# 122 products that nothing reads, put behind the last product of a one-core network kernel

## The chip, the cores and the metric

The kernel runs on one core of one Trainium2 chip (trn2). The metric is the device time of one execution in microseconds (us), lower is better; times are medians over runs. A profiled execution also gives a span, from its first to its last instruction.

## The reference

Two network blocks are applied one after the other to 256 rows of 1024 numbers in fp32: the first with four feed-forward parts, a recurrent/mLSTM mixer and a sparse attention mixer, the second with a pooling and retention mixer and then a feed-forward of 16384 experts. Only the end matters here:

```python
    hf = modulate(rmsnorm_2(x, lp['norm_ffn_g']), sh2, sc2)
    x = x + g2 * peer_ffn(hf, lp['peer_wq'], lp['peer_keys'], lp['peer_u'], lp['peer_v'])
...
    return rmsnorm_2(x, final_g)
```

`peer_ffn` picks 16 experts for each row and head, takes `gelu(u[e] . h)` times the softmax weight, and sums those multiples of `v[e]`. The kernel does it densely: it multiplies the rows by all experts' `u`, multiplies by a weight matrix that is zero where an expert wasn't picked, and multiplies by all `v`.

## The kernel before

The program is written engine by engine. Each stage adds work to the queues of SyncE (SP, which issues the DMAs), GpSimd (POOL), TensorE (PE), ScalarE (ACT) and VectorE (DVE), and semaphores order them. One block of such queues is open until the end of the kernel; `Kernel.close` (L396 to L402) closes it (L398), clears the semaphores (L400) and puts one more barrier (L401). At L398 each engine has a DRAIN, which ends when the engine's own work has ended, and then signals; POOL collects the signals of all the others and lets them go on.

An fp32 product is made of three (L539 to L545): each operand is split into a high and a low part of type fp32r, and `product` issues high by high, high by low and low by high. In the rows these are L543, L544 and L545, with moving operands of 256 or 512 columns against a stationary 128 x 128 piece. Before each product the stationary operand is loaded (LDWEIGHTS, engine PEld in the rows), also where it is the same as before. Products of plain fp32 operands (`mm`, L1041, and direct calls) stand in the trace as two records for one call. Transposes are products against an identity, `ident`.

`settle_pace` (L2116 to L2120) issues two products of the identity read as 16-bit numbers, start and stop set, into a bank whose content is not read. It is called at places of the expert stage and of two others. `start` begins with 12 products of `self.ones` in plain fp32 (L755), one behind the other into one place of bank 0, start and stop set, which nothing reads either.

The expert stage is `peer` (from L2609). It streams 256 half tiles (`experts`, 512 KB each) through three raw buffers; ACT makes the high part and POOL the low part of each in `high` and `low`, two slots of 1024 columns each. `up(n)` makes the 128 products with `u`, `down(n)` those with `v`, into PSUM banks 4 to 7. `GA` holds the high and low part of the weighted activations, two slots of 256 columns; `cells[0]` of the change is its high part. The last half tile goes to a place of its own (`last_tile`), and its low part is made by DVE (L3167).

After `down(125)` the queue of PE ends with a loop over the four output banks (t, h): for each of them the products of experts 126 and 127, and a signal `banked`. What follows is on the other engines: DVE multiplies a bank by the gate (L3173) and adds it to `keep_x` (L3177), ACT squares and sums it (L2996), small operations make the mean, root and reciprocal (L3182, L3186, L3001, L3191), DVE, POOL and ACT scale the rows (L3193, L2745, L3015), and SP stores them in four DMAs (L2730) and waits until they have landed. These use the banks 0 and 4 to 7 and the SBUF places of `x`, `g2`, `O1` and `O2`. Nothing on PE follows the loop over the banks, except its DRAIN at L398.

Of the kernel before, what the change touches and what calls it, by code (L numbers as in the profile page):

```python
# [16 lines left out]
F32 = mybir.dt.float32  # L17
F32R = mybir.dt.float32r
F16 = mybir.dt.float16
# [5 lines left out]
P = 128  # L25
# [94 lines left out]
class Modulation:  # L120
# [86 lines left out]
    def row(self, act, bank, row):  # L207

        self.k.nc.scalar.activation(row, bank[:, :], ACT.Copy).then_inc(self.copied.sem, 1)
# [118 lines left out]
class Kernel:  # L328
# [706 lines left out]
    def mm(self, out, lhsT, rhs, start, stop):  # L1035


        if isinstance(lhsT, (tuple, list)):
            ins = self.product(out, lhsT, rhs, start, stop)
        else:  # L1040
            ins = self.nc.tensor.matmul(out, lhsT, rhs, start=start, stop=stop)  # L1041
        if self.owed:
            self.owed -= 1
            ins.then_inc(self.released.sem, 1)
        return ins
# [1070 lines left out]
    def settle_pace(self, out):  # L2116

        square = self.ident.bitcast(F16)[:, 0:P]
        for _ in range(2):
            self.nc.tensor.matmul(out, square, square, start=True, stop=True)  # L2120

    def gate_row(self, part, banks):

        for k in range(KD):
            last = self.nc.tensor.matmul(self.psum[banks[k // 4]][:, (k % 4) * P:(k % 4 + 1) * P],
                                         self.modT[:, 8 * part + k, 0:1].to_broadcast([P, P]), self.ident,
                                         start=True, stop=True)
        return last
# [491 lines left out]
    def peer(self):  # L2620
# [4 lines left out]
        nc, ps, G, mod = self.nc, self.psum, G_PEER, self.modulation  # L2625
# [8 lines left out]
        high = side("high", 2 * D, dt=F32R).rearrange("p (s n) -> p s n", s=2)  # L2634
        low = side("low", 2 * D, dt=F32R).rearrange("p (s n) -> p s n", s=2)
# [7 lines left out]
        GA = [side(f"GA{n}", 2 * T, dt=F32R).rearrange("p (b t) -> p b t", b=2) for n in ("high", "low")]  # L2643
# [8 lines left out]
        at = lambda name, kb, cols: Arena(nc, f"peerT_{name}", self.ring_end + 1024 * kb - 64 * (kb >= 16), self.keep)(name, cols)  # L2652
# [95 lines left out]
        def _(pe):  # L2748
# [54 lines left out]
            w = self.ring_tile(pe, G_QUERY, 0)  # L2803
# [59 lines left out]
            for t in range(TT):  # L2863
                for h in range(2):
                    if t == 0:
                        pe.wait_ge(*made_low.at(4 * N - 3 + h))
                    for n in (N - 2, N - 1):
                        if t == 0 and n == N - 1:
                            pe.wait_ge(*last_low.at(h + 1))
                        last = self.product(ps[4 + 2 * t + h][:, :], [cell(i, n)[:, t * P:(t + 1) * P] for i in range(2)],  # L2870
                                            [halves_of(N + n, i)[:, h * 512:(h + 1) * 512] for i in range(2)], False, n == N - 1)
                    last.then_inc(banked.sem, 1)

        @self.block.scalar
        def _(act):
# [541 lines left out]
```

## Time and profile before

| | before |
|---|---|
| median of 2 runs | 2036.33 us (2035.77 and 2036.88) |
| span of the profiled execution | 2033.8 us |
| PE busy | 2017.6 us (99%), 15634 products |
| PEld busy | 1905.9 us (94%) |
| DVE, ACT, POOL busy | 52%, 56%, 85% |
| DMA | 395.28 MB, mean 194 GB/s |

The median lies 2.5 us above the span, time that is spent around the first and last instruction. A busy share says how long an engine had work in hand, not that it ran at its peak. Where products follow each other, one lasts longer than the distance to the next one's start, since they are pipelined: the distance of starts is what a stream costs, and the duration is what the last of it takes to come out. Times of a row are from the start of the span.

### The profile page before, as it was taken

Reading aid. Unit: us, or ns where it says so; the run is one execution under the profiler, and the core shown is the slowest. Engines: PE = TensorE matmul, PEld = TensorE weight load, DVE = VectorE, ACT = ScalarE, POOL = GpSimd, SP = SyncE. Lnnn points to the kernel's source line nnn. Section 1 sums busy time; section 2 is a strip of 40 time slices with the busy share of each in tenths; the row PEclk is TensorE's granted clock in tenths of the full one; section 3 lists DMA queues with packets and bytes.
Section 4 is the critical chain, followed back from the end, with each engine's and each line's share of the span. In section 5 each row is a group of like instructions: output and inputs, shape, how many; then the busy total and the mean of one; then the engine's idle time right before and its main releaser. Section 6 shows DMA issues by size and latency. Waiting matters only on the chain.

```text
span 2033.8 us, 39076 instructions
## 1 busy us (share of the span) xinstructions
PE 2017.6 (99%) x15634; PEld 1905.9 (94%) x15634; DVE 1057.5 (52%) x1985; ACT 1146.8 (56%) x1951; POOL 1718.8 (85%) x991
## 2 busy tenths in 40 slices
PE   9999999999999999999999999999999999999998
PEld 9999999999999979999889999999999998888886
DVE  6865745555454465224754316997788522223223
ACT  6344874445434475444654545557888655555555
POOL 5999789998999757899766686798777799999997
PEclk9999999999999999999999999999999999999999
DMA  9565456666666523666454455355454556555554
GB/s 350 210 222 190 166 187 249 217 219 246 248 250 225 208 83 138 239 223 220 166 181 145 149 185 196 124 190 177 167 167 167 165 185 203 193 195 193 193 196 146
DMA packets 80756, 395.28 MB, mean 194 GB/s; under 512 B 11100, under 2 KB 12252, under 8 KB 52448
## 3 DMA queue, kind: packets, MB, share of 16 engines
q1 hardware_dynamic: 80608, 393.28, 55.0%
q8 instruction: 97, 1.59, 0.3%
q14 instruction: 51, 0.42, 0.1%
HBM read 392.19 MB, written 1.05 MB: 193 GB/s over the span
## 4 chain that ended last, share of the span: by engine, by line
PE 89%; POOL 5%; DVE 3%; issue 2%; ACT 1%; DMA 1%; SPq 0%; ACTq 0%; POOLq 0%; DVEq 0%
PE bank L543 28%; PE bank L544 27%; PE bank L545 27%; POOL ring_low L496 5%; PE bank L1041 2%; PE bank L2782 1%; PE bank L2783 1%; PE bank L1828 1%; PE bank L1875 1%; PE bank L1857 1%; DMA ring_raw<-in_stream 1%; ACT ring_high L478 0%; DVE ring_low L981 0%; DVE keep_red L2482 0%; DVE context_red L2482 0%
## 5 line engine op out<-in xcount | busy, mean ns | idle before, releaser
L496 POOL TENSOR_TENSOR ring_low<-ring_raw,ring_high 128x1024 fp32r<-128x1024 f32 (+1 forms) x408 | 1026.5, 2546 | 191.6 <-ACT ring_high L478 189.7
L2740 POOL TENSOR_TENSOR peerS_low<-peerS_raw,peerS_high 128x512 fp32r<-128x512 f32 x510 | 659.5, 1318 | 85.2 <-ACT peerS_high L2892 83.7
L543 PE MATMUL bank<-keep_xThigh,ring_high 128*128 128x256 f32 x2080 | 582.6, 280 | 1.1 <-DVE ring_low L968 0.6
L545 PE MATMUL bank<-keep_xThigh,ring_low 128*128 128x256 f32 x2080 | 577.2, 278 | 0.0
L544 PE MATMUL bank<-keep_xTlow,ring_high 128*128 128x256 f32 x2080 | 577.2, 277 | 0.0
L478 ACT ACTIVATE ring_high<-ring_raw 128x2048 fp32r<-128x2048 f32 x204 | 390.1, 1913 | 265.4 <-PE bank L545 245.6
L543 PEld LDWEIGHTS bank<-keep_xThigh,ring_high 128*128 128x128 f32 x2080 | 390.9, 188 | 4.6 <-issue 3.7
L544 PEld LDWEIGHTS bank<-keep_xTlow,ring_high 128*128 128x128 f32 x2080 | 391.9, 188 | 0.3
L545 PEld LDWEIGHTS bank<-keep_xThigh,ring_low 128*128 128x128 f32 x2080 | 391.0, 188 | 0.0
L2892 ACT ACTIVATE peerS_high<-peerS_raw 128x512 fp32r<-128x512 f32 x510 | 320.5, 629 | 119.8 <-PE bank L545 92.4
L543 PE MATMUL bank<-keep_xThigh,peerS_high 128*128 128x256 f32 x1024 | 287.9, 281 | 0.0
L544 PE MATMUL bank<-keep_xTlow,peerS_high 128*128 128x256 f32 x1024 | 284.3, 278 | 0.0
L545 PE MATMUL bank<-keep_xThigh,peerS_low 128*128 128x256 f32 x1024 | 284.1, 277 | 0.0
L3137 DVE TENSOR_TENSOR peerS_GAlow<-peerA_A,peerS_GAhigh 128x256 fp32r<-128x256 f32 x127 | 90.1, 710 | 252.5 <-ACT peerS_GAhigh L2924 252.5
L544 PE MATMUL bank<-peerS_low,peerS_GAhigh 128*128 128x512 f32 x508 | 197.9, 390 | 0.0
L545 PE MATMUL bank<-peerS_high,peerS_GAlow 128*128 128x512 f32 x508 | 197.9, 390 | 0.0
L543 PE MATMUL bank<-peerS_high,peerS_GAhigh 128*128 128x512 f32 x508 | 197.9, 390 | 0.0
L543 PEld LDWEIGHTS bank<-keep_xThigh,peerS_high 128*128 128x128 f32 x1024 | 192.7, 188 | 0.3
L544 PEld LDWEIGHTS bank<-keep_xTlow,peerS_high 128*128 128x128 f32 x1024 | 192.9, 188 | 0.0
L545 PEld LDWEIGHTS bank<-keep_xThigh,peerS_low 128*128 128x128 f32 x1024 | 192.4, 188 | 0.0
L994 DVE TENSOR_TENSOR bank<-bank,keep_R 128x512 f32<-128x512 f32 x44 | 30.8, 700 | 245.3 <-PE bank L545 245.1
L933 ACT ACTIVATE ffn_silu<-bank 128x512 f32<-128x512 f32 x44 | 26.4, 599 | 166.6 <-DVE bank L994 166.6
(562 smaller groups left out, 3800.4 us busy)
## 6 DMA issues: line engine op xcount, KB each, us to landing
ring_raw<-in_stream SPq DMA_DIRECT2D x215, 1024.0 KB, 4.8
peerS_raw<-in_experts SPq DMA_DIRECT2D x256, 512.0 KB, 3.6
modcols_w<-in_ada_cols SPq DMA_DIRECT2D x32, 512.0 KB, 5.8
modlate_w<-in_ada_cols SPq DMA_DIRECT2D x8, 512.0 KB, 5.7
modcols_rows<-in_cond_rows SPq DMA_DIRECT2D x3, 1024.0 KB, 6.9
start_x<-in_x SPq DMA_DIRECT2D x2, 512.0 KB, 4.3
ring_raw<-in_stream SPq DMA_DIRECT2D x4, 256.0 KB, 5.8
context_in<-in_ctx SPq DMA_DIRECT2D x1, 1024.0 KB
```

The source lines that it names most:

```text
L478: self.nc.scalar.activation(self.parts(n)[0][:, cut], self.raw_slot(n)[:, cut], ACT.Copy).then_inc(self.high_done.sem, 1)
L496: self.nc.gpsimd.tensor_tensor(low_[:, cut], self.raw_slot(n)[:, cut], high[:, cut].bitcast(F32), ALU.subtract).then_inc(done.sem, 1)
L543: mm(out, sh, mh, start=start, stop=False)
L544: mm(out, sh, ml, start=False, stop=False)
L545: return mm(out, sl, mh, start=False, stop=stop)
L933: s_.activation(sg, pair(i, 0), ACT.Silu).then_inc(silu.sem, 1)
L994: v_.tensor_tensor(pair(i, 0), pair(i, 0), over, ALU.mult).then_inc(scaled.sem, 1)
L1041: ins = self.nc.tensor.matmul(out, lhsT, rhs, start=start, stop=stop)
L1828: last = nc.tensor.matmul(ps[4 + b][:, 0:P] if t == 0 else ps[4 + b][:, P:384], qT[rows, c, t * P:(t + 1) * P], kT[br][rows, c // 4, 0:(t ...
L2740: g_.tensor_tensor(low[:, m % 2, cut], xraw[:, m % 3, cut], high[:, m % 2, cut].bitcast(F32), ALU.subtract).then_inc(made_low.sem, 1)
L2892: s_.activation(halves_of(m, 0)[:, cut], xraw[:, m % 3, cut], ACT.Copy).then_inc(made_high.sem, 1)
L3137: v_.tensor_tensor(cell(1, n), A[:, n, :], cell(0, n).bitcast(F32), ALU.subtract).then_inc(gal.sem, 1)
```

## The change

Behind the loop over the output banks, PE gets 122 more products. Each sets start and stop and writes bank 1 or 2, which nothing reads from there on; nothing waits for them and they wait for nothing. They read `high`, `low`, `GA` and `ident` as they stand. Counted from the diff: five rows of 8 products with 512 moving fp32r columns (in order; two slots in turns in blocks of 16 columns; in turns in blocks of 4; every second column; the same two columns 256 times), 8 products of 16-bit numbers with 256 columns, six rows of 10 with 256 fp32r columns that begin at column 0, 4, 16, 32, 64 and 128 of `high`, one row of 10 with a stationary operand out of `low`, and 4 products in plain fp32 with 256 columns.

```diff
+    def unread_products(self, cells, high, low):
+
+
+        ps, mm = self.psum, self.nc.tensor.matmul
+        w = cells[0][:, 0, 0:P]
+        flat = high.rearrange("p s n -> p (s n)")
+        two = high.rearrange("p s (b c) -> p b s c", c=16)[:, 0:16]
+        lines = high.rearrange("p s (b c) -> p b s c", c=4)[:, 0:64]
+        ident = self.ident.bitcast(F16)
+
+        def row(count, out, weights, moving):
+            for _ in range(count):
+                mm(out, weights, moving, start=True, stop=True)
+
+        row(8, ps[1][:, :], w, flat[:, 0:512])
+        row(8, ps[2][:, :].rearrange("p (b s c) -> p b s c", s=2, c=16), w, two)
+        row(8, ps[1][:, :].rearrange("p (b s c) -> p b s c", s=2, c=4), w, lines)
+        row(8, ps[2][:, :], w, flat[:, 0:1024:2])
+        row(8, ps[1][:, :], w, flat[:, 0:2].unsqueeze(1).to_broadcast([P, 256, 2]))
+        row(8, ps[2][:, 0:256], ident[:, 0:P], ident[:, 0:256])
+        for at in (0, 4, 16, 32, 64, 128):
+            row(10, ps[1 + at // 4 % 2][:, 0:256], w, flat[:, at:at + 256])
+        row(10, ps[1][:, 0:256], low[:, 0, 0:P], flat[:, 0:256])
+        row(4, ps[2][:, 0:256], w.bitcast(F32), flat[:, 0:256].bitcast(F32))
...
                     last.then_inc(banked.sem, 1)
+            self.unread_products(GA, high, low)
```

## Rows read from the trace of the kernel before

**Rows 1.** The page: busy time, share of the span, instructions; chain by engine and line
```profile
PE 2017.6 (99%) x15634; PEld 1905.9 (94%) x15634; DVE 1057.5 (52%) x1985; ACT 1146.8 (56%) x1951; POOL 1718.8 (85%) x991
...
PE 89%; POOL 5%; DVE 3%; issue 2%; ACT 1%; DMA 1%; SPq 0%; ACTq 0%; POOLq 0%; DVEq 0%
```

**Rows 2.** Timeline of the end: start us, us, engine line op out<-in
```profile
2024.36 0.40 PE L544 MATMUL bank<-peerL_last,peerG_GA3high 128*128 128x512 f32 x1
...
2024.37 0.69 DVE L3177 TENSOR_TENSOR keep_x<-keep_x,bank 128x512 f32<-128x512 f32 x1
2024.59 0.40 PE L545 MATMUL bank<-peerL_last,peerG_GA3low 128*128 128x512 f32 x1
...
2025.77 0.75 DVE L3177 TENSOR_TENSOR keep_x<-keep_x,bank 128x256 f32<-128x256 f32 x2
...
2028.04 1.33 ACT L3015 ACTIVATE keep_x<-keep_x,keep_stat 128x512 f32<-128x512 f32 x2 [0.16 <-issue]
```

**Rows 3.** Source view of L398, the block's end: duration ns min/median/max, first and last start us
```profile
L398 PEldq DRAIN  x1: 4358/4358/4358, 2020.7 to 2020.7; - x1
...
L398 SPq DRAIN  x1: 7/7/7, 2032.4 to 2032.4; - x1
```

**Rows 4.** SP's own waits from 2015 us on: us in total, times, longest
```profile
SPq L398 <- DMA out<-keep_x: 2.1, 1, 2.1
```

**Rows 5.** PE alone in three stretches: busy (x instructions), granted clock, DMA share, GB/s
```profile
28.00:48.00 20.00, 20.00 (x171) 1.00 0.88 325
...
575.00:650.00 75.00, 75.00 (x664) 1.00 0.65 233
...
1750.00:1950.00 200.00, 200.00 (x884) 1.00 0.59 194
```

**Rows 6.** Timeline of PE, 1602 to 1604 us: 16-bit products, then fp32r ones
```profile
1603.19 0.22 PE L2783 MATMUL bank<-peerU_col,peerU_low 128*128 128x128 f16 x1
1603.24 0.22 PE L2782 MATMUL bank<-peerU_col,peerU_high 128*128 128x128 f16 x1
1603.30 0.22 PE L2783 MATMUL bank<-peerU_col,peerU_low 128*128 128x128 f16 x1
1603.33 0.36 PE L543 MATMUL bank<-keep_xThigh,peerS_high 128*128 128x256 f32 x1
1603.53 0.28 PE L544 MATMUL bank<-keep_xTlow,peerS_high 128*128 128x256 f32 x1
1603.65 0.28 PE L545 MATMUL bank<-keep_xThigh,peerS_low 128*128 128x256 f32 x1
```

**Rows 7.** Timeline of PE, 1116 to 1119 us: products in plain fp32
```profile
1116.68 1.03 PE L1041 MATMUL bank<-mix_vn_vn,mix_PTb_PTb 128*128 128x256 f32 x4
1117.54 1.03 PE L1041 MATMUL bank<-mix_S_S,mix_qd_qd 128*128 128x256 f32 x4
```

**Rows 8.** Groups of PE and PEld by line and shape: count, busy us, mean ns
```profile
L543 PE MATMUL bank<-keep_xThigh,ring_high 128*128 128x256 f32 x2080 | 582.6, 280 | 1.1 <-DVE ring_low L968 0.6 <-DVE keep_xTlow L3073 0.5
...
L545 PE MATMUL bank<-peerS_high,peerS_GAlow 128*128 128x512 f32 x508 | 197.9, 390 | 0.0
...
L2798 PE MATMUL bank<-peerT_xs_xs,keep_ones 128*128 128x256 f32 x16 | 3.7, 386 | 0.3 <-ACT peerT_xs_xs L2928 0.3
...
L2120 PE MATMUL bank<-keep_ident 128*128 128x128 f16 x24 | 3.4, 223 | 0.0
```

**Rows 9.** Tile views of two stationary operands of 64 columns, PEld: ns min/median/max
```profile
L1041 PEld LDWEIGHTS bank<-ring_raw,nsa_cmpX0first x16: 193/196/219, 690.7 to 693.8; 128*64 128x64 f32 x16
...
L1875 PEld LDWEIGHTS bank<-nsa_PT,nsa_vv x128: 132/137/138, 739.2 to 776.9; 128*64 128x64 f32 x128
```

**Rows 10.** Engines in two stretches of the end: busy (x), then PEclk, DMA share, GB/s
```profile
2018.00:2025.00 7.00, 6.30 (x27) 4.45 (x25) 6.43 (x10) 1.86 (x5) 2.55 (x2) 1.00 0.00 0
2025.00:2027.00 2.00, 0.00 (x0) 0.00 (x0) 1.93 (x7) 1.53 (x6) 1.05 (x1) 1.00 0.00 0
2027.00:2034.00 7.00, 0.00 (x0) 0.00 (x0) 1.52 (x5) 1.73 (x5) 0.22 (x1) 0.68 0.40 151
```

**Rows 11.** Timeline of PE, first 8 us and 1608 us: plain fp32, 128 columns
```profile
1.07 4.99 PE L755 MATMUL bank<-keep_ones 128*128 128x128 f32 x24 [1.07 <-POOL keep_ones L746]
...
1608.86 1.95 PE L2125 MATMUL bank<-keep_ident,keep_modT 128*128 128x128 f32 x16
```

**Rows 12.** Groups of PEld by line and shape: count, busy us, mean ns
```profile
L544 PEld LDWEIGHTS bank<-peerS_low,peerS_GAhigh 128*128 128x128 f32 x508 | 95.4, 188 | 19.6
...
L2782 PEld LDWEIGHTS bank<-peerU_col,peerU_high 128*128 128x128 f16 x256 | 24.2, 97 | 1.1
```

## The prediction

> **What bounds the kernel now.** I read the page first: PE is busy 99% of the span and holds 89% of the chain that ended last [rows 1]. So over the whole kernel nearly every product on PE's queue costs its own distance. But the change puts its products where PE has nothing more to do, so what counts is the end, and there I read the timeline and the block's end. The last product starts at 2024.59 and lasts 0.40 us [rows 2]. PE's DRAIN at L398 starts at 2020.7 and lasts 4.358 us, so PE is done at 2025.1 [rows 3]. The others are not: DVE adds the last pieces from 2025.77 on, ACT scales rows until 2028.04 + 1.33 = 2029.4 [rows 2], and SP then waits 2.1 us for the stores to land [rows 4]. SP's DRAIN ends at 2032.4 [rows 3], and it is the last of the five. From there to the end of the span are 2033.8 - 2032.4 = 1.4 us of barrier and semaphore clearing, which begin only when the last engine has drained, whichever that is. PE therefore has a free stretch of 2032.4 - 2025.1 = 7.3 us. What it does beyond that moves the end one for one.
>
> **The change part by part.** Nothing is removed or moved, and no wait, DMA or work on another engine is added; no queue but PE's gets an instruction, and on PE nothing stands behind the new products but the DRAIN. The cost is the stream of 122 products, less 7.3 us. The distance of starts is what each costs:
>
> - 512 columns of fp32r. In a long run of such products 884 records touch 200 us [rows 5]; two of them only reach in at the edges, so 200/882 = 0.227 us each. At the end of the kernel, after DVE's late low part, they stand a little wider: from 2024.36 to 2024.59 is 0.23 us [rows 2]. The wider pace also shows for 256 columns, where 20 us at the start of the kernel hold 171 records, 0.118 us each, against 75/662 = 0.1133 in the long run [rows 5], a factor of 1.04. The new products follow the last ones without a gap, so I take the wider pace, 0.231: 40 x 0.231 = 9.24 us.
> - 8 products of 16-bit numbers, 256 columns. With 128 columns starts lie 0.055 us apart, 1603.19 to 1603.24 to 1603.30 [rows 6]; twice the columns, 0.111: 0.89 us. The step back to fp32r costs something once: that product starts at 1603.33 and the next only at 1603.53, 0.20 instead of 0.12 [rows 6]. 0.09 us.
> - 70 products of 256 columns of fp32r, six rows at different beginnings and one with another stationary operand. After 16-bit products the kernel before runs at the narrow pace (that is what `settle_pace` is called between), so 70 x 0.1133 = 7.93 us [rows 5]. At the wide pace it would be 8.3. Which columns of a buffer a contiguous read starts at is something the kernel before varies all the time, in both operands, at one mean duration of 277 to 280 ns [rows 8]. I take no surcharge for it.
> - 4 products in plain fp32, 256 columns. L2798 is called 8 times and stands as 16 records [rows 8], so a call is two. Four records go from 1116.68 to 1117.54, 0.215 each [rows 7]. 8 x 0.215 = 1.72 us.
>
> The sum is 9.24 + 0.89 + 0.09 + 7.93 + 1.72 = 19.9 us, of which 7.3 lie under the tail of the others: +12.6 us. PE drains at 2025.1 + 19.9 = 2045.0, and the span goes from 2033.8 to 2046.4. The median of the runs stands 2.5 us above the span of the profiled execution, and its two runs 1.1 us apart; the same step from the median gives 2036.33 + 12.6 = 2048.9 us, or +0.6%.
>
> **What the trace does not show** is a moving operand that isn't contiguous; all that I see on PE are plain runs. Four of the five rows of 512 columns are not: blocks of 16, blocks of 4, every second column, two columns over and over. The nearest row is a strided stationary operand. `nsa_cmpX0first` is loaded in 64 columns that lie 8 numbers apart and takes 196 ns, against 137 ns for 64 columns in a row [rows 9]: 59/64 = 0.92 ns for each column that isn't beside the one before. As an upper bound I let each break in a moving operand cost that. Every second column: 512 breaks, 0.47 us a product, 3.8 for 8. Two columns over and over: 256 breaks, 1.9. Blocks of 4: 128 breaks, 0.9. Blocks of 16: 32 breaks, 0.2. Together 6.8 us, and 2055.7 us in all. The lower bound is a little under the sum, since a read of two columns over and over could also be spared whatever makes an fp32r product 0.227 long where one of plain fp32, which streams as many steps in two passes of 256 columns, takes 0.215 [rows 5, 7]: 40 x 0.016 = 0.6 us less, 2048.3. I take no surcharge, since breaks alone do not make the price: a contiguous load of 128 columns takes 188 ns and one of 64 takes 137 [rows 12, 9], 0.8 ns a column, while a contiguous moving operand runs at 0.227/512 = 0.44 ns a column [rows 5]. The two paths have different rates, and the moving one must be fed faster anyhow. But both ends stay in the range.
>
> The Trainium skill has a rule on this (Advanced Engine Details and Errata, Memory Cachelines): SBUF is read in lines of 16 bytes, and two hits in a line are enough for the full rate. By it the strided load of the 64 columns, one hit a line, should be slow, and the trace agrees (196 against 137 ns); all moving patterns of this change have two hits or more, and the sum would stay as it is. A reading of the same rule by which two hits are just half of what a moving operand needs makes the second rival below.
>
> **The rivals.**
>
> 1. *The stream at the rates above*: 2048.9 us, and with small errors of the pace (0.4 us), of the switch between types and of the median (0.6 us) 2047.6 to 2050.2. For it: every rate is from long runs of the same kernel, and PE waits for nobody. 0.64.
> 2. *Reads that fetch anew cost more.* The row of every second column takes twice its time, 8 x 0.231 = 1.8 us more (2050.7), perhaps that of the two repeated columns too (2052.6), and by the upper bound 2055.7. For it: the strided load [rows 9]. Against it: the moving path's own rate. 0.24.
> 3. *The clock falls.* The granted clock is 1.00 as long as PE works and the mean over 2027 to 2034, where PE has been idle since 2025, is 0.68 [rows 10], a fall from 2.4 to 1.2 GHz. In the first microseconds 24 records take 4.99 us, 0.21 each, where later 16 of the same shape take 1.95, 0.11 each [rows 11]. If the clock were low throughout, the stream would be 39.8 us, +32.5, 2068.8 us. Against it: the new products follow the old without a gap, so PE doesn't idle. 0.05.
> 4. *The change does nothing*, because products whose result isn't read are dropped or because they hide. Time 2036.3. Against it: the 24 unread products of L2120 stand in the trace [rows 8], and 19.9 is well over 7.3. 0.04.
> 5. *The other side, over 2% slower: products do not overlap when each starts a bank anew.* The new ones overwrite the same bank 8 or 10 times in a row, and should each have to wait for the last to come out before it loads its weights, each would cost load and duration: 40 x (0.188 + 0.390) = 23.1, 70 x (0.188 + 0.277) = 32.6, 8 x about 0.37 = 3.0 for the 16-bit ones (0.097 + 0.220 for 128 columns, and 0.05 for the others), 8 x (0.190 + 0.380) = 4.6; 63.3 us in all [rows 8, 12], +56.0, 2092.3 us. It passes 2% (40.7 us) when the stream takes 48.0 us, 0.39 us a product. Against it: L755 does just that, and its 24 records in 4.99 us leave no room for load and duration one behind the other [rows 11]. 0.02.
>
> Left over is 0.01, for which I can name nothing and which I give to faster.
>
> **How the numbers follow.** The likeliest is the first: 2048.9 us. Its own range is 2047.6 to 2050.2. The range for 8 in 10 takes in the lower bound and most of the second rival, to short of its far end: 2047.4 to 2054.0. Two per cent is about what a measurement of this kernel can tell from no change. Rivals 1 to 4 lie within it (0.6%, 1% at the most, 1.6%, 0): 0.97. Slower by more is the fifth, 0.02; faster 0.01.
>
> **What would show it.** In the profile of the changed kernel PE should be busy to about 2044.8 with no gap behind 2024.6, and PE's DRAIN at L398 should end last, near 2045.0, while SP's has still ended at about 2032.4. PE and PEld should have 118 + 8 = 126 records more, 15760. The starts in the five rows of 512 columns should all lie 0.231 us apart; the second rival shows in the fourth and fifth, where they would be near 0.46, or a few hundredths wider in the third. After the 16-bit row the distances should be 0.113, the same for all six beginnings. The granted clock should stay 1.00 until some microseconds behind 2045. DVE, ACT and POOL should have the times that they had: in the tail before, DVE's L3177 took 0.69 us beside PE at work [rows 2], and 12 us of cover now lie over them.
>
> The prediction is wrong if a kind of product costs more than its row here says, which its starts would show, or if the end of the block costs more when PE comes last than when SP does; the distance from PE's DRAIN to the end of the span, 1.4 us here, would show that.

## The result and the profile after

The changed kernel takes 2051.35 us (median of 2 runs, 2049.3 and 2053.39) against 2036.33 before: a ratio of 1.0074, interval 1.0058 to 1.009. The span of its profiled execution is 2047.5 us, 13.7 above the 2033.8 of before. By the line of 2% nothing has changed; by its own interval the kernel is slower by some 15 us.

First the page's busy line, which answers to [rows 1]:

```profile
PE 2038.7 (100%) x15760; PEld 1922.5 (94%) x15760; DVE 1067.1 (52%) x1985; ACT 1146.9 (56%) x1951; POOL 1722.1 (84%) x991
```

The block's end, source view of L398 (duration ns min/median/max, first and last start us), for [rows 3]:

```profile
L398 SPq DRAIN  x1: 7/7/7, 2031.3 to 2031.3; - x1
L398 PEldq DRAIN  x1: 3092/3092/3092, 2043.0 to 2043.0; - x1
```

SP's own waits (us in total, times, longest), for [rows 4]:

```profile
SPq L398 <- PEq L398: 14.9, 1, 14.9
...
SPq L398 <- DMA out<-keep_x: 2.1, 1, 2.1
```

126 records have come, as many as 118 products and 4 calls of two records make. SP has drained at 2031.3 as it did before, 7.8 us after the start of the last product of the loop (2023.55, below; 2024.59 and 2032.4 before, [rows 2, 3]). PE drains at 2043.0 + 3.1 = 2046.1, and SP now waits 14.9 us for it. From there to the end of the span are 1.4 us, as before. In this execution the loop ended 1.0 us earlier than in the one of before, for no reason that the change holds (the queue up to there is the same), which is why the spans are 13.7 apart and the stream less its cover, below, 14.8.

The timeline of PE shows that the new products follow without a gap. Behind it are the stretches, which give what each row costs. They are cut at the first start of each row of the change: in order, blocks of 16, blocks of 4, every second column, two columns over and over, 16-bit, the 70 of 256 columns, plain fp32. Columns are busy us (x records touched), granted clock, DMA share, GB/s; the length of a stretch is the row's cost.

```profile
2023.55 0.39 PE L545 MATMUL bank<-peerL_last,peerG_GA3low 128*128 128x512 f32 x1
2023.78 11.29 PE L2134 MATMUL bank<-peerS_high,peerS_GAhigh 128*128 128x512 f32 x40
2034.90 1.05 PE L2134 MATMUL bank<-keep_ident 128*128 128x256 f16 x8
2035.71 7.39 PE L2134 MATMUL bank<-peerS_high,peerS_GAhigh 128*128 128x256 f32 x60
...
2044.13 1.89 PE L2134 MATMUL bank<-peerS_high,peerS_GAhigh 128*128 128x256 f32 x8
```

```profile
2023.78:2025.62 1.84, 1.84 (x8) 1.00 0.00 0
2025.62:2027.54 1.92, 1.92 (x9) 1.00 0.16 63
2027.54:2029.54 2.00, 2.00 (x9) 1.00 0.68 256
2029.54:2033.13 3.59, 3.59 (x9) 1.00 0.30 118
2033.13:2034.91 1.78, 1.78 (x10) 1.00 0.00 0
2034.91:2035.71 0.80, 0.80 (x10) 1.00 0.00 0
2035.71:2044.13 8.42, 8.42 (x73) 1.00 0.01 2
2044.13:2045.86 1.73, 1.73 (x10) 1.00 0.00 0
sum 22.08, PE 22.08; mean PE 2.76
```

The stream is 22.1 us, not 19.9. 1.75 us of the difference are one row, every second column. (A product counts as touched in two stretches where it reaches over the cut, so the counts add up to more than 126.)

### The profile page after: what moved, and what is told of

It reads as the page before. It is cut to its first block, busy times and chain, and to the rows that moved or that the text cites. A ratio compares the mean times of both kernels' runs of the same rounds, so it can differ in the third digit from the quotient of the medians.

```text
span 2047.5 us, 39328 instructions
## 1 busy us (share of the span) xinstructions
PE 2038.7 (100%) x15760; PEld 1922.5 (94%) x15760; DVE 1067.1 (52%) x1985; ACT 1146.9 (56%) x1951; POOL 1722.1 (84%) x991
## 4 chain that ended last, share of the span: by engine, by line
PE 87%; POOL 7%; DVE 2%; issue 2%; ACT 1%; DMA 1%; SPq 0%; POOLq 0%; DVEq 0%; ACTq 0%
PE bank L543 26%; PE bank L545 26%; PE bank L544 26%; POOL ring_low L496 5%; POOL peerS_low L2765 3%; PE bank L1041 2%; PE bank L2134 1%; PE bank L2807 1%; PE bank L2808 1%; PE bank L1828 1%; PE bank L1875 1%; PE bank L1857 1%; ACT ring_high L478 0%; DVE ring_low L981 0%; DMA ring_raw<-in_stream 0%
## 5 line engine op out<-in xcount | busy, mean ns | idle before, releaser
L3163 DVE TENSOR_TENSOR peerS_GAlow<-peerA_A,peerS_GAhigh 128x256 fp32r<-128x256 f32 x127 | 99.5, 784 | 244.0 <-ACT peerS_GAhigh L2950 244.0
```

Of the source, the lines that this page charges most:

```text
L3163: v_.tensor_tensor(cell(1, n), A[:, n, :], cell(0, n).bitcast(F32), ALU.subtract).then_inc(gal.sem, 1)
```

## The experiments

Where distances of starts are given with three decimals, they are the usual difference between neighbouring starts in that row; (n - 1) of them and the duration of the last make up the length of the merged row that is shown. `lines`, `lines2`, `pace` and `regions` were executed once each; they are read by these distances and not by their total times. The ratios are the measurement's own, over all its executions, and can differ in the fourth decimal from that of the two medians.

**The free stretch.** 28 products in order in place of the 122:

```diff
-        row(8, ps[1][:, :], w, flat[:, 0:512])
...
-        row(4, ps[2][:, 0:256], w.bitcast(F32), flat[:, 0:256].bitcast(F32))
+        for _ in range(28): mm(ps[1][:, :], w, flat[:, 0:512], start=True, stop=True)
```

> Only 28 products of 512 columns in order in place of the 122. At 0.231 us each the stream is 6.5 us long, less than the 7.3 us for which PE has drained before SP. Theory A, free stretch: PE's DRAIN at L398 ends before SP's, the span is that of the kernel before within 0.3 us, and the ratio to before is 1.000 within its interval. Rival: unread products beside the tail slow DVE, ACT or the stores, or PE's stream costs from its first product on: +1 us or more, up to 6.5 (ratio 1.0005 to 1.003).

Measured: 2037.86 us against 2037.38 for the kernel before in the same comparison, a ratio of 1.0004, interval 0.9995 to 1.0013. Its timeline and the block's end:

```profile
2026.53 0.39 PE L545 MATMUL bank<-peerL_last,peerG_GA3low 128*128 128x512 f32 x1
2026.77 6.53 PE L2127 MATMUL bank<-peerS_high,peerS_GAhigh 128*128 128x512 f32 x28
```

```profile
L398 PEldq DRAIN  x1: 4242/4242/4242, 2029.1 to 2029.1; - x1
...
L398 SPq DRAIN  x1: 7/7/7, 2034.3 to 2034.3; - x1
```

28 products last 6.5 us and are gone before SP has drained, 7.8 us behind the start of the last product of the loop, as in the trace before (2034.3 and 2026.53 here): the theory of the free stretch holds. PE's DRAIN ends at 2029.1 + 4.2 = 2033.3, 1.0 us before SP's. The interval would not have shown a cost of 1 us, but the tail between the two starts is the same length, and that shows that none of it was slowed.

That length is not fixed, though. It is 7.8 us in eight of the ten traces, but 9.6 in `pace` (2034.7 - 2025.03) and 9.7 in `regions` (2033.2 - 2023.51), two runs described below. In both, SP waits 3.9 and 4.0 us for the stores to land where it waits 2.1 in the others, and in both a transfer of 16 KB of instructions (queue q8) comes while the stores are under way, beside one of 8 KB that every trace has there. SP's wait in `pace`, and the queue of that transfer in the window from 2030 to 2035 us (packets, MB, share of 16 engines):

```profile
SPq L398 <- DMA out<-keep_x: 3.9, 1, 3.9
```

```profile
...
q8 instruction: 1, 0.02, 1.2%
```

In the changed kernel the 16 KB come at 2036 us, behind the stores (they are the 2 GB/s in the stretch from 2035.71 on), and `short` has none behind its loop. So the cover of 7.3 us held for the changed kernel, but another stream of products can stretch it: PE is done 0.5 us after the loop's last start, and in these two the cover was 9.1 and 9.2 us, with a tail 1.9 us longer for all. That the transfer makes the stores late is read from these two coincidences and not tested.

**The same again, twice over, and without the dear row.** `again` is the changed kernel with more runs; the other two:

```diff
             self.unread_products(GA, high, low)
+            self.unread_products(GA, high, low)
```

```diff
-        row(8, ps[2][:, :], w, flat[:, 0:1024:2])
```

> The changed kernel once more, with more rounds. Its stream is 22.1 us long in the trace, so the step from before should be 22.1 - 7.3 = 14.8 us less what varies in where the last product of the loop starts (1.0 us earlier in the changed kernel's trace): 13.8 to 14.8 us, ratio 1.0068 to 1.0073. Rival: the step of 15.0 us between the medians of two runs each (1.0074) holds something beside the stream, and the ratio is 1.0078 or more.

> The 122 products twice. One for one beyond the free stretch: the stream is 44.2 us, the step from before 44.2 - 7.3 = 36.9 us, ratio 1.0181. If the end of the block had a cost of its own when PE comes last, or the first microseconds of the stream were dearer, the step would differ from twice 22.1 less 7.3 by that. If the clock fell in it, it would be longer by up to 22 us for each 22 us at the low clock.

> The changed kernel without its fourth row, the 8 products of every second column. The row took 3.6 us in the trace. Theory A (the row costs what its starts say): PE's DRAIN ends 3.6 us earlier relative to the last product of the loop, the stream is 18.5 us, and the step from before 11.2 us, ratio 1.0055. If the row only cost what a row in order does (1.85 us) and the rest came from elsewhere, the step would be 12.9 us, ratio 1.0063.

| | stream by theory | ratio by theory | ratio measured | PE drained behind the loop's last start |
|---|---|---|---|---|
| again | 22.1 us | 1.0068 to 1.0073 | 1.0073 (1.0059 to 1.0087) | 22.5 us |
| double | 44.2 | 1.0181 | 1.0182 (1.0165 to 1.0199) | 44.5 |
| no_step | 18.5 | 1.0055 | 1.0052 (1.0035 to 1.0069) | 18.9 |

The last column is PE's DRAIN less the start of the loop's last product, in us of each trace: 2045.1 + 3.1 - 2025.67 for `again`, 2067.0 + 3.1 - 2025.55 for `double`, 2039.8 + 3.1 - 2024.02 for `no_step`, and 2046.1 - 2023.55 = 22.5 for the changed kernel. The second helping of 122 products adds 22.0 us, one for one, with the clock at 1.00; the row of every second column is worth 3.6. `double` also settles whether the stores, which move during the rows of blocks and of every second column, made these dear: in the second helping no store is left, and the rows take 1.92, 2.00 and 3.59 us again. The interval of `no_step` (7 us wide) holds the rival's 1.0063 as well, and that of `again` its rival's 1.0078; it is the traces that decide. Against something beside the stream in `again` speak its DRAIN, 22.5 us behind the loop's last start, with 1.5 us from there to the end of its span (2049.7 - 2048.2). Loops that end at 2023.55 in one execution and at 2026.53 in another, in the same code, say why a median of a few can't: that spread, 3.0 us, is nearly as large as the row.

**What a moving operand costs by its pattern.** In place of the 122 products, rows of 8 (or 4 calls in plain fp32) that differ in what is moved; some of the lines:

```diff
...
+        for _ in range(8): mm(ps[2][:, :], w, flat[:, 2:514], start=True, stop=True)
+        for _ in range(8): mm(ps[1][:, :].rearrange("p (a b) -> p a b", b=2), w, pairs, start=True, stop=True)
+        for _ in range(8): mm(ps[1][:, :], w, flat[:, 0:1536:3], start=True, stop=True)
+        for _ in range(8): mm(ps[2][:, :], w, flat[:, 0:2048:4], start=True, stop=True)
+        for _ in range(8): mm(ps[1][:, 0:256], w, flat[:, 0:2048:8], start=True, stop=True)
...
+        for _ in range(8): mm(ps[2][:, :], ident[:, 0:P], some(8, 16), start=True, stop=True)
```

> In place of the 122 products: 12 rows of 8 with moving operands of other patterns (fp32r, then 16-bit), and 3 rows of 4 in plain fp32. What is read is the distance of starts in each row. Theory A, groups: the moving operand comes in aligned groups of four fp32 numbers (16 bytes), and a product takes the larger of its columns' time and about 1.76 ns for each group that it has to fetch (0.450 us over 256 groups in the changed kernel). Per product: in order 0.231; in order from the third number on 0.231; two of each four 0.45; blocks of four that lie across two groups 0.45; step 3 (384 groups) 0.68; step 4 (512) 0.90; step 8 with 256 columns 0.45; one column over and over 0.22; 16-bit in order 0.22, step 2 (128 groups) 0.22 to 0.25, step 4 (256) 0.45, step 8 (512) 0.90; plain fp32 records of 256 columns: in order 0.216, step 2 (128 groups) 0.22, step 4 (256) 0.45. Theory B, breaks: each column that isn't beside the one before costs 0.43 ns more, wherever it lies. Then: two of each four 0.34; blocks of four across two groups 0.25 as in the changed kernel; steps 3 and 4 0.45 like step 2; step 8 with 256 columns 0.23; one column over and over 0.45; 16-bit steps 2, 4 and 8 all 0.43.

The timeline of PE in `lines`, one merged row for each kind, in the order of the expectation: in order, from the third number on, two of each four, blocks of four across two groups, steps 3, 4 and 8, one column over and over, 16-bit steps 1, 2, 4 and 8, plain fp32 steps 1, 2 and 4:

```profile
2026.65 2.00 PE L2136 MATMUL bank<-peerS_high,peerS_GAhigh 128*128 128x512 f32 x8
2028.48 2.04 PE L2137 MATMUL bank<-peerS_high,peerS_GAhigh 128*128 128x512 f32 x8
2030.36 3.79 PE L2138 MATMUL bank<-peerS_high,peerS_GAhigh 128*128 128x512 f32 x8
2033.96 2.84 PE L2139 MATMUL bank<-peerS_high,peerS_GAhigh 128*128 128x512 f32 x8
2036.63 3.77 PE L2140 MATMUL bank<-peerS_high,peerS_GAhigh 128*128 128x512 f32 x8
2040.22 3.86 PE L2141 MATMUL bank<-peerS_high,peerS_GAhigh 128*128 128x512 f32 x8
2043.90 1.92 PE L2142 MATMUL bank<-peerS_high,peerS_GAhigh 128*128 128x256 f32 x8
2045.65 1.93 PE L2143 MATMUL bank<-peerS_high,peerS_GAhigh 128*128 128x512 f32 x8
2047.41 1.90 PE L2144 MATMUL bank<-keep_ident 128*128 128x512 f16 x8
2049.15 1.97 PE L2145 MATMUL bank<-keep_ident 128*128 128x512 f16 x8
2050.96 3.77 PE L2146 MATMUL bank<-keep_ident 128*128 128x512 f16 x8
2054.55 7.38 PE L2147 MATMUL bank<-keep_ident 128*128 128x512 f16 x8
2061.75 3.60 PE L2148 MATMUL bank<-peerS_high,peerS_GAhigh 128*128 128x256 f32 x8
2065.14 2.41 PE L2149 MATMUL bank<-peerS_high,peerS_GAhigh 128*128 128x256 f32 x8
2067.38 3.77 PE L2150 MATMUL bank<-peerS_high,peerS_GAhigh 128*128 128x256 f32 x8
```

Neither theory stands. Theory A (groups of four, a price for each) is right for two of each four (0.451 for 0.45), for one column over and over (0.219), for the 16-bit rows (0.226, 0.451, 0.900) and for plain fp32 in steps 2 and 4 (0.226, 0.451), and wrong for steps 3 and 4 in fp32r (0.450 and 0.460 for 0.68 and 0.90), for step 8 (0.218 for 0.45) and for blocks across two groups (0.331 for 0.45). Theory B (a price for each break) has steps 3, 4 and 8 of fp32r right and 16-bit step 4 nearly (0.43 for 0.451), and pairs (0.34), blocks across groups (0.25), one column over and over (0.45) and 16-bit steps 2 and 8 (0.43 each) wrong. So the second run tested whether it goes by the kind of number, or whether the small operand of the 16-bit rows, read up to 16 times, made them dear:

```diff
+        for _ in range(8): mm(ps[1][:, :], w16, half[:, 0:2048:4], start=True, stop=True)
+        for _ in range(8): mm(ps[2][:, :].rearrange("p (a b) -> p a b", b=32), w, again, start=True, stop=True)
...
+        for _ in range(8): mm(ps[2][:, :], w16, half[:, 0:4096:8], start=True, stop=True)
+        for _ in range(40): mm(ps[1][:, 0:256], w, flat[:, 0:256], start=True, stop=True)
```

> In place of the 122 products: rows of other moving operands, to mend what the run of read patterns left. There fp32r products of 512 columns took 0.45 us for steps 2, 3 and 4 alike, but 16-bit ones 0.226, 0.451 and 0.900 for steps 2, 4 and 8, over a small operand read 4 to 16 times. Theory C, kind: in fp32r a step costs double whatever its size, and in 16-bit the time goes with the bytes stepped over from 8 bytes on (16 bytes a column: 0.90), because 16-bit numbers are taken in other portions. Then 16-bit steps 2, 4, 8 over a long operand are again 0.226, 0.451, 0.900, and fp32r step 4 over 128 columns read 16 times is 0.46. Theory D, the small operand: reading the same few hundred bytes again is what costs, and the long 16-bit row of step 8 is 0.45 while the fp32r row over 128 columns is 0.90. Further rows: fp32r step 16 with 128 columns 0.11 by C; blocks of four aligned columns, four left out, 0.25 as the alternating blocks of the change; pairs that lie across two groups of four 0.45 (a group each) to 0.90; plain fp32 records with 256 columns in order 0.216, step 2 0.226, step 4 0.451. The clock: in that run it fell to 1.2 GHz from 4 us after the start of the 0.900 row on, and the plain fp32 records behind it took 0.427. If a stream of starved products lowers it, it falls here too during or behind the row of step 8, the 40 products of 256 columns behind it take 0.213 us at first and 0.120 later, and the plain fp32 rows, which here stand in front, take 0.216.

The rows of `lines2` that decide, by its timeline: plain fp32 in order, step 2 and step 4; fp32r step 4 over 128 columns, 16 times; 16-bit step 8 over 4096 numbers; then 40 products in order.

```profile
2026.65 1.89 PE L2134 MATMUL bank<-peerS_high,peerS_GAhigh 128*128 128x256 f32 x8
2028.37 1.98 PE L2135 MATMUL bank<-peerS_high,peerS_GAhigh 128*128 128x256 f32 x8
2030.19 3.77 PE L2136 MATMUL bank<-peerS_high,peerS_GAhigh 128*128 128x256 f32 x8
...
2040.52 4.28 PE L2140 MATMUL bank<-peerS_high,peerS_GAhigh 128*128 128x512 f32 x8
...
2051.99 7.36 PE L2145 MATMUL bank<-peerS_high,keep_ident 128*128 128x512 f16 x8
2058.31 6.94 PE L2146 MATMUL bank<-peerS_high,peerS_GAhigh 128*128 128x256 f32 x40
```

The small operand is not it: the long 16-bit row of step 8 stands at 0.900 again and the small fp32r one at 0.461. The theory of the kind of number holds. Put as the cost of one column at the high clock (distance over columns; a plain fp32 call is two records, here one of them):

| bytes from column to column | 2 | 4 | 8 | 12 | 16 | 32 | 64 |
|---|---|---|---|---|---|---|---|
| 16-bit, ns | 0.42 | 0.44 | 0.88 | | 1.76 | | |
| plain fp32, ns | | 0.84 | 0.88 | | 1.76 | | |
| fp32r, ns | | 0.44 | 0.88 | 0.88 | 0.90 | 0.85 | 0.88 |

At the steps measured, plain fp32 and 16-bit cost the larger of the column's own time and 0.11 ns for each byte stepped over. fp32r doubles with the first step and stays there. Why fp32r stops at 0.88 and the others don't, the runs do not say; the others were not tried beyond 16 bytes. The last entry is weaker than the rest: its products have only 128 columns (0.113 us each), there is no row in order of that size beside it, and each has a load of weights of 0.19 us in its time, which may set the distance as well. Blocks in fp32r: pairs cost 0.88 a column wherever they lie (0.451 for two of each four, 0.453 for pairs across two groups). Four aligned with four left out cost 0.233 a product (0.25 expected), no more than a row in order, though blocks of four in turns from two slots cost 0.250 and, across groups, 0.331.

**The clock.** PEclk in `lines2`: in front of the 0.900 row, in its first part, in its later part, at the first and at the later ones of the 40 products:

```profile
2046.00:2050.00 4.00, 4.00 (x13) 1.00 0.00 0
2052.00:2054.80 2.80, 2.80 (x6) 1.00 0.00 0
2054.90:2057.90 3.00, 3.00 (x4) 0.51 0.00 0
2058.50:2061.70 3.20, 3.20 (x13) 0.50 0.00 0
2061.90:2062.70 0.80, 0.80 (x9) 1.00 0.00 0
```

As in `lines` (below), the granted clock goes from 1.00 to 0.50 (2.4 to 1.2 GHz) inside the row of step 8, while PE is busy for all of it by the records. In `lines` that row goes from 2054.55 to 2061.75:

```profile
2058.00:2061.00 3.00, 3.00 (x5) 0.70 0.00 0
2061.00:2064.00 3.00, 3.00 (x8) 0.50 0.00 0
```

The products of that row keep their 0.900 at both levels, so it is not the array's clock that paces them, and the operand is the likely cause; the 256-column ones behind it take 0.213 at the low level and 0.118 to 0.124 after it. In `lines` the plain fp32 records behind that row took 0.427, in `lines2`, ahead of it, 0.216. Rows at 0.45 did not lower it: in `lines` fp32r steps 3, 4 and 8, all at 0.85 to 0.90 ns a column, follow each other for 9.0 us (2036.63 to 2045.65) with the clock at 1.00. That the slow row itself lowers the clock rests on two falls in two runs, and on none in the traces that lack such a row; no run varies its length.

**Why 0.120 and not 0.113.** `pace` and `regions` put rows of 256 columns behind a `settle_pace` pair:

```diff
+        pair()
+        for n in range(20): mm(ps[2][:, 0:256], w, flat[:, 0:256], start=True, stop=True)
...
+        for n in range(10): mm(ps[1][:, 0:256], own, x, start=True, stop=True)
```

> In place of the 122 products: rows of 10 or 20 fp32r products with 256 columns, most behind a pair of 16-bit products of 128 columns (the kernel's own settle_pace). Asked is why the rows behind the 16-bit ones stood 0.120 us apart in the changed kernel where the kernel's long runs have 0.1133. Theory A, the pair: two 16-bit products of 128 columns bring the narrow distance within a few products, and eight with 256 columns did not. Then all rows behind a pair run at 0.1133 after at most five products, and only the first row, without a pair, at 0.118 to 0.120. Theory B, the stream: products of one kind with one stationary operand that start their bank anew keep 0.118 to 0.120 behind a pair too, and one of the rows that come closer to the kernel's own products (two banks in turns, summing up in one bank, two stationary operands in turns, stationary out of high with moving out of xT, moving operands of other places) comes down to 0.1133 and names what it hangs on. Theory C, chance of the phase: rows differ without a pattern.

Measured: behind a pair the rows come to 0.120, as the row without one does, and stay there for 20 products. Two banks in turns, summing up, two stationary operands in turns and other places in `high` change nothing. Only the row with `high` stationary and `xT` moving came down, to 0.113 from its sixth product on. That is theory B, with the place of the operands as what it hangs on, and `regions` took the places apart:

```diff
+        for n in range(16): mm(ps[2][:, 0:256], far, flat[:, 0:256], start=True, stop=True)
+        pair()
+        for n in range(16): mm(ps[1][:, 0:256], far, x, start=True, stop=True)
```

> In place of the 122 products: seven rows of 16 fp32r products of 256 columns, each behind a settle_pace pair, with the stationary and the moving operand in the lower part of the memory (high, GA) or in the upper one (xT). Theory A, one stream apart: the distance is 0.1133 when the two operands lie in different parts and 0.120 when in the same, so high with xT, xT with high, GA with xT and xT with GA come to 0.1133, and xT with xT, GA with high and high with high stay at 0.120. Theory B, the moving operand: rows that move xT come to 0.1133 (high, xT and GA as stationary), all that move high or GA stay at 0.120, whatever is stationary. Theory C, the one buffer: only high as stationary with xT moving, the pair of the kernel's own products, comes to 0.1133.

Its timeline: `high` with `xT`, `xT` with `high`, `xT` with itself, `GA` with `xT`, `GA` with `high`, `high` with itself, `xT` with `GA` (stationary first):

```profile
2023.84 2.13 PE L2132 MATMUL bank<-keep_xThigh,peerS_high 128*128 128x256 f32 x16
...
2025.90 2.13 PE L2134 MATMUL bank<-peerS_high,keep_xTlow 128*128 128x256 f32 x16
...
2027.97 2.15 PE L2136 MATMUL bank<-keep_xThigh,keep_xTlow 128*128 128x256 f32 x16
...
2030.06 2.13 PE L2138 MATMUL bank<-keep_xThigh,peerS_GAhigh 128*128 128x256 f32 x16
...
2032.13 2.15 PE L2140 MATMUL bank<-peerS_high,peerS_GAhigh 128*128 128x256 f32 x16
...
2034.22 2.16 PE L2142 MATMUL bank<-peerS_high 128*128 128x256 f32 x16
...
2036.31 2.13 PE L2144 MATMUL bank<-peerS_GAhigh,keep_xTlow 128*128 128x256 f32 x16
```

The split is that of theory A: operands in different parts of the memory stand at 0.118 in the end, operands in the same part at 0.120. But the place isn't all, for in the changed kernel the rows that begin at columns 16 and 32 stand at 0.118 too, with both operands in the same part. And theory A's number failed: none of the four rows reached 0.1133 within 16 products, the very pair that did in `pace` included. What brings a stream to the narrow distance is open. It is worth 0.007 us a product, 0.5 us here.

## Why the prediction was right, and where not

- *PE's stream decides, less what lies under the tail.* Right, and shown from both sides: 28 products cost nothing that can be seen, 244 cost twice the stream less the same cover. With the measured stream the step is 22.1 - 7.3 = 14.8 us; measured were 15.0 (two runs each), and in `again` a ratio of 1.0073, 14.9 us, with 14.2 between the medians (2051.55 and 2037.38).
- *512 columns in order, 9.24 us for 40 at one price.* The price held for the row in order (1.85 predicted, 1.84 measured) and for what repeats two columns (1.78). Blocks of 16 cost 1.92, blocks of 4 2.00. The step that failed is "I take no surcharge" for every second column: 3.59 for 1.85. My reason, that the moving path must be fed faster than the stationary one, was true for reads in order and said nothing about steps. The second rival had this very time for that row (1.8 us more) and was wrong about the repeated columns and about its upper bound (3.8 more). The lower bound's 0.016 us a product is 0.231 less 0.215; with the 0.227 of its sentence it would be 0.012.
- *Page and measurement.* The rule that I cited from the Trainium skill (Advanced Engine Details and Errata, Memory Cachelines), two hits in a line of 16 bytes for the full rate, does not hold for TensorE's moving fp32r operand: every second column has two hits in a line and takes 0.450 us for 0.231. The measurement decides. Nor does it for 16-bit numbers 8 bytes apart, which have two hits as well and take 0.451 for 0.216. It holds for 16-bit numbers 4 bytes apart (0.226), which have four, and for plain fp32 8 bytes apart (0.226 for 0.216 a record), which have two.
- *70 products of 256 columns, 7.93 us, with 0.09 for the change of type.* 8.42 measured, 0.118 to 0.120 each in place of 0.1133; the term was too small by 0.4 us. I had tied the narrow pace to the 16-bit products in front, and `pace` shows that these don't bring it. That the beginning of a contiguous read costs nothing worth counting was right: the first of the seven rows took 1.28 us, with the change of type, and the others 1.18 to 1.20. The 0.09 for that change were for nothing here: the last 16-bit product is followed after 0.027 us and the first fp32r one after 0.201, together what 0.109 and 0.120 make.
- *16-bit, 0.89 us, and plain fp32, 1.72.* 0.80 and 1.73.
- *The other engines keep their times, and the block's end costs 1.4 us whoever is last.* Right. Beside the new products DVE's last L3177, now L3203, takes 0.76 us for two halves (0.75 before), ACT's L3015, now L3041, 1.35 (1.33), and POOL's L2745, now L2770, 1.30 (1.27). DVE's total is 9.6 us more, but 9.4 of that are the low part of `GA` (L3137, now L3163: 0.784 us each for 0.710), all ahead of the change.
- *The median's 2.5 us above the span.* The profiled execution of the changed kernel took 2049.3 us, 1.8 above its span, and so do those of `again` and `double` (1.7 and 1.8). The rest of my 2.5 was the scatter of the runs, and the same scatter is why a step of 14.8 and one of 13.7 in the spans are no contradiction.
- *Two products that overwrite a bank don't overlap* fell as expected: in `pace` the row that sums up in one bank and the rows that start anew both stand at 0.120.

So the direction, the mechanism and the range were right; of the 2.2 us by which the stream was longer, 1.75 are one row's rate that the trace before did not show, and 0.4 a pace taken from a neighbouring stretch; what else was off by some 0.1 us (the blocks up, the repeated columns and the 16-bit row down) nearly cancels.

## What to carry to other kernels

Work put behind the last useful instruction of an engine costs its stream less the time by which that engine was done early; so read the DRAINs of the block's end before anything else. See also whether the added instructions bring a transfer of instructions that falls among the stores: that may make the tail itself longer, as the 1.9 us in `pace` and `regions` suggest. Keep the operand that streams through PE contiguous, in runs of four fp32 numbers or more that begin at a multiple of four: one column of two costs double the time in fp32r, and one 16-bit number in each 16 bytes four times, and behind such a row the clock was low in both runs that had one. A rate taken from a long run is good to some 6% elsewhere in the same kernel (0.120 for 0.1133).

## What the hardware showed unasked

Beside the table above: the granted clock halved under a stream in which PE never paused by the records, 2.9 us after the start of the row at 0.900 us a product in `lines2` and 4.7 us after it in `lines`, and for some microseconds the products after it paid 0.09 us each with 256 fp32r columns (0.213 for 0.120), and 0.21 a record in plain fp32 (0.427 for 0.216). A product in plain fp32 with every second column costs almost nothing more (0.226 for 0.216 a record), where the fp32r product doubles. A call is two such records, 0.45 us for 256 columns; fp32r, at 0.88 ns a column, would take 0.23 for as many (an estimate from the rows of 512), so its lead shrinks from nearly four times to two.
